# Banded attention scores of the first query block: split products against full-precision ones

## What is computed

```python
# banded_attention(q, k, v, t5_table, window=128, sinks), 16 query heads, 4 key heads, width 64
# queries in blocks of 128; each block reads its own 128 keys and the 128 before them
s = einsum('bgrnqd,bgnkd->bgrnqk', qb, kb) * (Dh ** -0.5)
valid = (dist >= 0) & (dist < window) & (kpos >= 0)
s = where(valid, s + bias, NEG)
p = softmax(concatenate([s, sink]))[..., :-1]
o = einsum('bgrnqk,bgnkd->bgrnqd', p, vb)
```

## Time and profile before

| | us |
|---|---|
| time, median of 3 | 1212.67 |
| lowest, highest | 1212.18, 1212.84 |
| the profiled execution | 1212.38 |
| its span in the trace | 1210.5 |
| TensorE busy | 1202.1 |
| VectorE busy | 833.7 |
| ScalarE busy | 495.8 |

### The profile page before, as it was taken

How to read it: one execution, slowest core, us unless ns; L and a number is a source line. 1 busy time by engine, 2 the same in 40 slices (tenths; PEclk the granted TensorE clock), 3 DMA queues, 4 the chain that set the end, 5 groups by cost and what they waited for, 6 DMA issues and landing times.

```text
span 1210.5 us, 16101 instructions
## 1 busy us (share of the span) xinstructions
PE 1202.1 (99%) x5720; PEld 995.1 (82%) x5720; DVE 833.7 (69%) x1303; ACT 495.8 (41%) x795; POOL 7.5 (1%) x18
## 2 busy tenths in 40 slices
PE   9999999999999999999999999999999999999998
PEld 8888888888888888888887888888888888887786
DVE  6868897797889987553367866566654444778862
ACT  7544333232333323552244534334433332355643
POOL 0000000000000000000000000000000000000000
PEclk9999999999999999999999999999999999999999
DMA  8533232222222232243322232232233534221211
GB/s 325 175 106 103 87 104 87 71 87 87 70 87 89 102 105 87 87 175 104 104 87 87 87 104 89 102 104 101 90 110 105 175 105 139 88 71 53 74 67 70
DMA packets 35843, 125.54 MB, mean 104 GB/s; under 512 B 4080, under 2 KB 5760, under 8 KB 35536
## 3 DMA queue, kind: packets, MB, share of 16 engines
q1 hardware_dynamic: 33424, 116.41, 28.4%
q0 software_dynamic: 928, 6.08, 1.5%
q10 hardware_dynamic: 1440, 2.36, 0.6%
HBM read 122.72 MB, written 4.21 MB: 105 GB/s over the span
## 4 chain that ended last, share of the span: by engine, by line
PE 99%; DMA 0%; DVE 0%; ACT 0%; issue 0%; ACTq 0%; DVEq 0%
PE acc L870 80%; PE acc L887 3%; PE side L1223 2%; PE acc L1223 2%; PE acc L892 1%; PE acc L954 1%; PE acc L1187 1%; PE side L1148 1%; PE acc L907 1%; PE side L1020 1%; PE side L1040 1%; PE side L971 1%; PE acc L971 1%; PE acc L942 1%; PE acc L1159 1%; DMA par<-params 0%
## 5 line engine op out<-in xcount | busy, mean ns | idle before, releaser
L1257 DVE TENSOR_TENSOR w_low<-w_raw,w_high 128x1024 fp32r<-128x1024 f32 x213 | 257.7, 1221 | 41.7 <-ACT w_high L485 38.5
L485 ACT ACTIVATE w_high<-w_raw 128x1024 fp32r<-128x1024 f32 x213 | 221.1, 1050 | 69.4 <-PE acc L870 53.4
L870 PE MATMUL acc<-h_high,w_high 128*128 128x512 f32 x880 | 218.1, 390 | 0.0
L870 PE MATMUL acc<-h_low,w_high 128*128 128x512 f32 x880 | 217.4, 389 | 0.0
L870 PE MATMUL acc<-h_high,w_low 128*128 128x512 f32 x880 | 217.3, 389 | 0.0
L870 PEld LDWEIGHTS acc<-h_low,w_high 128*128 128x128 f32 x880 | 165.2, 188 | 34.4
L870 PEld LDWEIGHTS acc<-h_high,w_low 128*128 128x128 f32 x880 | 165.2, 188 | 34.3
L870 PEld LDWEIGHTS acc<-h_high,w_high 128*128 128x128 f32 x880 | 164.6, 188 | 33.9
L1332 DVE SCALAR_TENSOR_TENSOR convs<-long_u,par,convs 128x510 f32<-128x510 f32 (+28 forms) x232 | 170.3, 734 | 6.6
L1542 DVE TENSOR_TENSOR gate<-acc,gate 128x512 f32<-128x512 f32 x16 | 11.1, 692 | 53.7 <-PE acc L870 52.1
L870 PE MATMUL acc<-f_high,w_high 128*128 128x512 f32 x176 | 43.9, 390 | 0.0
(11 more groups left out here) (341 smaller groups left out, 1737.9 us busy)
## 6 DMA issues: line engine op xcount, KB each, us to landing
w_raw<-weights SPq DMA_DIRECT2D x213, 512.0 KB, 3.2
x_in<-x SPq DMA_DIRECT2D x4, 512.0 KB, 10.1
x<-x POOLq DMA_DIRECT2D x1, 2048.0 KB, 8.5
rows_dram<-strip_dram POOLq DMA_DIRECT2D x1, 2048.0 KB, 11.5
w_raw<-weights SPq DMA_DIRECT2D x4, 384.0 KB, 7.1
mem_in<-mem ACTq DMA_DIRECT2D x4, 256.0 KB, 7.2
bias<-rows_dram POOLq DMA_DIRECT2D x1, 1024.0 KB, 7.0
out<-result ACTq DMA_DIRECT2D x4, 256.0 KB, 2.6
```

What stands on the lines that cost most here:

```text
L485: act.activation(w_high[:, s, :], raw[s][:, :], ACT.Copy).then_inc(weight_high, 1)
L870: mm = pe.matmul(acc[:, bank, 0:width], w[:, s, (skip + b) * P:(skip + b + 1) * P], moving[v][:, k, :], start=first and b == 0 and w is w_ ...
L1257: dve.tensor_tensor(w_low[:, s, :], raw[s][:, :], w_high[:, s, :].bitcast(F32), ALU.subtract)\
```

## The change

For the steps of the first block (n = 0) the three split products of each pair are replaced by one product of float32 operands. These operands are two new tiles, `q2_first` (8 x 128 elements a partition) and `k2_first` (2 x 128). VectorE makes them anew from the split parts, as the sum of high and low, in a new function `first_block(p)`: one sum for the four query tiles of p, one for the key tile. It is called twice in VectorE's list, behind the `root_low` of result 8 (p = 0) and of result 9 (p = 1). The new tiles lie where `x2` and later `o2` lie, so `first_block` waits for `y_ready`, whose products read `x2`. `scores` of steps 0 and 1 wait for `second_first` 2, steps 8 and 9 for 4.

```diff
+        q2_first = sb("q2_first", [P, KT, P], F32, 56)
+        k2_first = sb("k2_first", [P, 2, P], F32, 60)
...
                 pe.wait_ge(second_low, KT + 1 + p)
+                if n == 0:
+                    pe.wait_ge(second_first, 2 * p + 2)
                 at_least(pe, sw_step, 6 * (step - 2) + 4)
                 for i in range(2):
                     j = 2 * half + i
+                    for e in range(2) if n == 0 else ():
+                        at = 64 * e
+                        mm = pe.matmul(side[:, 2 * (step % 2) + e, MEM * i + P:MEM * i + MEM],
+                                       q2_first[at:at + 64, 4 * p + j, :], k2_first[at:at + 64, p, :],
+                                       start=True, stop=True)
                     for o, (query, key) in enumerate(((q2_high[:, 4 * p + j, :], k2_high), (q2_high[:, 4 * p + j, :], k2_low),
-                                                      (q2_low[p][:, j, :], k2_high))):
+                                                      (q2_low[p][:, j, :], k2_high)) if n else ()):
...
+            def first_block(p):
+
+                dve.wait_ge(y_ready, KT)
+                dve.wait_ge(second_low, KT + p + 1)
+                dve.tensor_tensor(q2_first[:, 4 * p:4 * p + 4, :], q2_high[:, 4 * p:4 * p + 4, 0:P].bitcast(F32),
+                                  q2_low[p][:, :, 0:P].bitcast(F32), ALU.add).then_inc(second_first, 1)
+                dve.tensor_tensor(k2_first[:, p, :], k2_high[:, p, 0:P].bitcast(F32), k2_low[:, p, 0:P].bitcast(F32),
+                                  ALU.add).then_inc(second_first, 1)
...
                     if 2 <= k <= KT + 2:
                         root_low(k - 1)
+                    if KT < k <= KT + 2:
+                        first_block(k - KT - 1)
```

More of the change, by code:

```diff
@@ L325, in build @@
         second_low = sem("second_low")
+        second_first = sem("second_first")
         first_scaled = sem("first_scaled")
@@ L1143, in scores @@
                     j = 2 * half + i
+                    for e in range(2) if n == 0 else ():
[3 more added lines that the diff above has]
+                                       start=True, stop=True)
                     for o, (query, key) in enumerate(((q2_high[:, 4 * p + j, :], k2_high), (q2_high[:, 4 * p + j, :], k2_low),
-                                                      (q2_low[p][:, j, :], k2_high))):
+                                                      (q2_low[p][:, j, :], k2_high)) if n else ()):
                         for e in range(2):
                             at = 64 * e
-                            mm = pe.matmul(side[:, 2 * (step % 2) + e, MEM * i + P * blocks[0]:MEM * i + MEM],
+                            mm = pe.matmul(side[:, 2 * (step % 2) + e, MEM * i:MEM * i + MEM],
                                            query[at:at + 64, n * P:(n + 1) * P],
-                                           key[at:at + 64, p, (n - 1 + blocks[0]) * P:(n + 1) * P],
+                                           key[at:at + 64, p, (n - 1) * P:(n + 1) * P],
                                            start=o == 0, stop=o == 2)
```

## The result

| | us |
|---|---|
| before, median of 10 executions | 1212.42 (1212.16 to 1212.84) |
| changed, median of 10 executions | 1214.70 (1213.74 to 1216.77) |
| ratio | 1.0019, 95% interval 1.0011 to 1.0027 |
| the changed kernel's profiled execution | 1214.11, span 1212.3 |

The changed kernel is slower by 2.3 us. The ten executions don't lie around the median but in groups: five from 1213.74 to 1214.11, four from 1215.29 to 1215.43, one at 1216.77. The median is the middle of the gap between 1214.11 and 1215.29, where no execution lies. Those of the first group have a mean granted clock of TensorE of 0.999 or 1.000, the others 0.996 to 0.999; the mean alone doesn't tell them apart. Before, all ten are within 0.7 us.

The account below looks back on a forecast made before the run. TensorE, busy 99% of the span, was taken to bound the kernel. + 1.76 us (scores(3)) - 0.40 (steps 8 and 9) = + 1.36 on the median 1212.67 gave 1214.0 us; range 1212.9 to 1216.0.

Parts of the forecast that it names:

- The place: Both first_block calls stand in VectorE's gapless stretch ahead of biased(0); scores(3) is released 0.08 us before TensorE wants it.
- The cost of the sums: Each first_block call on VectorE takes 0.60 + 0.21 + 0.11 = 0.92 us, both 1.84.
- The allowance of 0.05 a call: For the range, up to 0.05 us more per first_block call, for two semaphore waits ahead of each first sum.
- The release of scores(3): TensorE's weight load for scores(3) starts 0.05 us after VectorE's last read of biased(1); TensorE is 1.76 us late from there.
- The products: Full-precision pairs 0.11 us apart, 0.44 a step; steps 8 and 9 save 0.40, steps 0 and 1 save 0.46, given back.
- The rule on four passes: Skill rule against the change: true FP32 takes four passes, the split three products; by count alone + 2.2 us.
- The sum: For the whole kernel, + 1.76 at scores(3) - 0.40 at steps 8 and 9 = + 1.36 us on 1212.67: 1214.0.
- The clock: Rival: TensorE's clock falls to 1.2 GHz in the new hole, slowing rows behind scores(3) by 1.9 us: 1215.9; chance 0.19.
- the rivals: Clock falls 1215.9 (0.19); heads don't overlap 1214.8 (0.08); sums hidden 1211.8 (0.05); later wait eats steps 8 and 9, 1214.4.
- the heads without overlap: Rival: the two heads' full-precision products don't overlap, 0.87 us a step; 1212.67 + 1.76 + 0.4 = 1214.8; chance 0.08.
- a full granted clock throughout: Expected sign in the changed trace: TensorE's granted clock stays full despite the new hole, 2.1 us of 2.8.
- Nothing behind it gave the delay back or added to it: Behind scores(3) TensorE waits for nobody and all engines move as a block; turn(0) comes at 1083.3.

Follow-up runs that it names:

- the sums alone: The kernel before with only the two first_block calls on VectorE, results unused, products still split, no new TensorE wait; median 1214.62 us of 9.
- the changed kernel again: The changed kernel, unaltered, executed once more for another profile; 1215.51 us.
- one wait: The changed kernel with first_block waiting for second_low alone, so its first sum carries one semaphore instead of two; 1215.15 us in one execution.
- a longer pause: The changed kernel with first_block(1) done three times in a row, writing the same values again; 1217.28, 1218.29, 1218.51 and 1218.90 us.

## Why the prediction was right, and where it wasn't

- **The place.** VectorE's gapless stretch and the slack of under 0.1 us at scores(3) decide, as said; the sums alone made the whole delay. The waits came where they were forecast, 0.95 and 1.12 us where 0.8 and 1.3 stood, none at scores(0).
- **The cost of the sums** was 0.99 us a call, forecast 0.92. The sums themselves were right (0.61 and 0.20); the gap ahead was 0.10 and not 0.03, since two semaphores stand there (0.03 with one). The allowance of 0.05 a call was just too small.
- **The release of scores(3)** was 0.12 us from the last read to the weight load (1076.80 to 1076.92), forecast 0.05 from the earlier trace rows, where one semaphore is waited for and not two; that this is the reason wasn't tested. With 0.12 the slack before was not 0.08 but about 0.01. Together TensorE is 1.99 us late, not 1.76.
- **The products.** Pairs of records 0.11 apart, the two heads at once: 16 records in 1.16 us. 0.43 us saved within steps 8 and 9, forecast 0.40, of which 0.34 arrive at the end. Steps 0 and 1 saved 0.39 and not 0.46: from the first pair's start to the last it is 1.16 - 0.27 = 0.89 for seven distances of 0.11, so the first load stands open for about 0.1 and not 0.05; it changed nothing, as that saving was lost anyway. The full-precision products of half the rows do overlap, as those of half the columns do.
- **The rule on four passes** (the Trainium skill, FP8 and Floating Point Precision, TensorE Precision Notes) is borne out in what it counts: two records for each product, and a pair of them (0.11 us for 128 columns) takes about as long as a pair of split products of twice the columns (0.12 for 256). The runs contradict only what one would conclude from it for three split products at 128 columns, since those cost nearly as much as at 256: 0.112 us a pair. That their weights hold them up is read from these rows; no run varied the loads.
- **The sum**, 1214.0, is near the time of the cheap group (median 1213.88), in part by luck. The difference was forecast as 1.36; the trace has 1.66 (1.99 for 1.76 and 0.34 for 0.40), the group 1.46. And it was put on 1212.67, the median of three, where that of ten was 1212.42: 0.25 too high a base made up for too small a difference.
- **The clock** was the rival and not the forecast. Its mechanism and place were right and its size nearly (1.5 us, forecast 1.9; 3.4 us at the low level, where the earlier trace rows gave 4.6), its chance was not: 0.19 was meant for a fall in most executions, and it came in half, five of ten. That moved the median to 1214.7, between the two and above the band of 1213.6 to 1214.5 that the forecast had for itself; that it lies in the wide range is owed to the rivals, which the range took in. (That 1214.7 is next to the 1214.8 of the heads without overlap is chance: the timelines refute that rival.) The step that failed is "a full granted clock throughout", and behind it the reading of the earlier trace rows: a pause of 1.24 us without a fall, and a full clock for 1.90 us behind the last product and half after that. No single pause is longer than that 1.24 (0.95 and 1.12), and one of 1.12 alone did nothing; only the two together, 2.1 us with scores(2) between them, brought the fall, and that sum does not lie between 1.24 and 1.90, as the prediction has it, but above. And the question was put as either - or, where half of the executions have the fall and half don't. What decides between them no run shows.
- **Nothing behind it gave the delay back or added to it**, as the earlier trace rows had said: turn(0) came 2.15 us later, which is the 0.15 from ahead of scores(0) and the 2.0.

## What to carry to other kernels

Work that is added to an engine with much idle time still costs its full length when it stands in a stretch without a gap that ends in a result the bounding engine is about to want. Look for the stretch's release and its slack, not for the engine's share of busy time; here the same sums cost 2.0 us in one place, 0.2 when all but one small sum stand where VectorE is idle or ahead, and nothing when a w_low makes room for that one too. And a new pause of the bounding TensorE may cost more than its length, by half clock behind it, in some executions and not in others, and two short pauses close together can do what one of them doesn't: a change of that sort is judged by the groups its executions fall in, not by one profile.

## What the hardware showed that was not expected

- The same program has a full clock in one execution and, behind the same pause, 3.4 us at 1.2 GHz in the next (1213.9 and 1215.4 us). The low clock is seen in three profiles (the changed kernel again, one wait, a longer pause); the other counts go by the times. Two pauses of 0.95 and 1.12 us with under 1 us of work between them did it in 5 of 10 executions of the changed kernel and in the single one taken later, 0.80 and 1.11 in the single one with one wait, 0.55 and 1.12 in 4 of 9, one of 1.12 alone in none of eleven, and the pauses filled with products in none of eleven.
- The low clock can come behind the pause: TensorE had been at work again since 1076.9 when the granted clock fell at 1077.6 (0.80 in the stretch 1077 to 1078). After the longer pause it was low with the first pair.
- Split products of 128 columns are hardly cheaper than those of 256 (0.112 against 0.12 us a pair), and at 128 columns one full-precision product, 0.22 us for a pair of heads, beats three split ones, 0.34.
- A second semaphore in front of an instruction costs VectorE 0.07 us when the other is met at the last moment (0.10 against 0.03 behind k_low).
